# One ScalarE copy for two PSUM tiles, and one broadcast product for four, in a gated delta rule

## What is computed

```python
decay = jnp.exp(jnp.where(causal, gc[..., :, None] - gc[..., None, :], -jnp.inf))
kb = k * beta[..., None]
lower = jnp.where(strict, jnp.einsum('nhcid,nhcjd->nhcij', kb, k) * decay, 0.0)
uw = lax.linalg.triangular_solve(lower, rhs, left_side=True, lower=True, unit_diagonal=True)
...
kd = k * jnp.exp(g_last[..., None] - gc)[..., None]
v_new = u_c - jnp.einsum('nhik,nhkv->nhiv', w_c, state)
state = state * a_c[..., None, None] + jnp.einsum('nhjk,nhjv->nhkv', kd_c, v_new)
```

## The kernel before

| step | level 2 | level 3 | level 4 | level 5 |
|---|---|---|---|---|
| 0 | 2 | 3 | 1 | 2 |
| 1 | 1 | 2 | 3 | 0 |
| 2 | 1 | 0 | 1 | 3 |
| 3 | 0 | 1 | 2 | 3 |
| 4 | 0 | 3 | 0 | 2 |
| 5 | 0 | 2 | 3 | 0 |
| 6 | 1 | 3 | 1 | 2 |
| 7 | 3 | 1 | 1 | 1 |

## Time and profile before

### The profile page before, as it was taken

One profiled execution on the slowest core, in us unless ns is written; L12 is line 12 of the kernel. 1 busy time (PEld: TensorE's weight loads), 2 busy tenths in 40 slices (PEclk: granted clock), 3 DMA queues, 4 the chain that ended last, 5 costly groups with the idle time before them and its releaser, 6 DMA issues. The chain is left out here.

```text
span 3287.1 us, 56382 instructions
## 1 busy us (share of the span) xinstructions
PE 3210.5 (98%) x23386; PEld 2744.4 (83%) x23386; DVE 1654.8 (50%) x2484; ACT 1286.7 (39%) x2064; POOL 62.5 (2%) x79
## 2 busy tenths in 40 slices
PE   8999999999999999999998999999999999999999
PEld 7997889889788988888887888788888888876899
DVE  7744574774457552223674667542233323247444
ACT  5433454544345452223543444432223222234433
POOL 0000000000000010000000000000000000000000
PEclk9999999999999999999999999999999999999999
DMA  6545654454655432222221333222222222211353
GB/s 260 180 167 220 227 189 169 180 179 157 253 205 180 178 116 102 93 99 90 103 78 64 131 118 131 79 103 90 102 90 90 90 102 90 102 64 39 129 180 127
DMA packets 62918, 439.27 MB, mean 134 GB/s; under 512 B 6672, under 2 KB 9872, under 8 KB 10000
## 3 DMA queue, kind: packets, MB, share of 16 engines
q1 hardware_dynamic: 61552, 435.43, 36.7%
q10 hardware_dynamic: 1184, 1.18, 0.1%
HBM read 435.54 MB, written 1.05 MB: 133 GB/s over the span
## 5 line engine op out<-in xcount | busy, mean ns | idle before, releaser
L701 ACT ACTIVATE sb_w_split<-sb_ring 128x2048 fp32r<-128x2048 f32 x263 | 504.2, 1917 | 905.4 <-PE ps_low L465 706.0
L709 DVE TENSOR_TENSOR sb_w_split<-sb_ring,sb_w_split 128x2048 fp32r<-128x2048 f32 x263 | 603.3, 2294 | 432.3 <-ACT sb_w_split L701 432.3
L465 PE MATMUL ps_low<-sb_x_split,sb_w_split 128*128 128x512 f32 (+1 forms) x3520 | 691.3, 355 | 18.6 <-DVE sb_w_split L735 13.4
L465 PE MATMUL ps_high<-sb_x_split,sb_w_split 128*128 128x512 f32 (+1 forms) x3520 | 685.2, 353 | 1.9 <-DVE sb_w_split L709 1.9
L465 PEld LDWEIGHTS ps_low<-sb_x_split,sb_w_split 128*128 128x128 f32 x3520 | 579.5, 189 | 119.6 <-DVE sb_w_split L735 13.4
L465 PEld LDWEIGHTS ps_high<-sb_x_split,sb_w_split 128*128 128x128 f32 x3520 | 580.1, 189 | 96.8 <-DVE sb_w_split L709 2.9
L465 PE MATMUL ps_low<-sb_a_split,sb_w_split 128*128 128x256 f32 (+1 forms) x2112 | 370.2, 325 | 0.0
L465 PE MATMUL ps_high<-sb_a_split,sb_w_split 128*128 128x256 f32 (+1 forms) x2112 | 368.2, 323 | 0.0
L465 PEld LDWEIGHTS ps_low<-sb_a_split,sb_w_split 128*128 128x128 f32 x2112 | 314.2, 190 | 37.6 <-DVE sb_w_split L709 2.8
L465 PEld LDWEIGHTS ps_high<-sb_a_split,sb_w_split 128*128 128x128 f32 x2112 | 314.2, 190 | 30.4
L465 PE MATMUL ps_low<-sb_xn,sb_ring 128*128 128x256 f32 (+1 forms) x800 | 184.3, 388 | 0.5 <-ACT sb_xn L2652 0.5
(11 more groups left out here) (376 smaller groups left out, 3181.0 us busy)
## 6 DMA issues: line engine op xcount, KB each, us to landing
sb_ring<-weights SPq DMA_DIRECT2D x411, 1024.0 KB, 4.8
sb_consts<-consts SPq DMA_DIRECT2D x1, 2020.0 KB, 14.9
sb_h<-xT SPq DMA_DIRECT2D x1, 1024.0 KB, 6.9
sb_h<-ctxT ACTq DMA_DIRECT2D x1, 1024.0 KB, 20.8
out<-sb_h SPq DMA_DIRECT2D x1, 1024.0 KB, 4.8
sb_vectors<-vectors SPq DMA_DIRECT2D x1, 269.0 KB, 2.9
sb_arena<-positions ACTq DMA_DIRECT2D x1, 128.0 KB, 7.1
```

The lines of the kernel that those rows point to most:

```text
L465: ins = self.g.nc.tensor.matmul(out, lhsT, rhs, start=start, stop=stop)
L701: g.nc.scalar.activation(g.w_split[:, 0, s % 2, :], g.ring[:, n % SLOTS, :], ACT.Copy).then_inc(g.sem["w_high"], 1)
L709: g.nc.vector.tensor_tensor(g.w_split[:, 1, s % 2, :], g.ring[:, n % SLOTS, :], g.w_split[:, 0, s % 2, :].bitcast(F32), ALU.subtract).then ...
```

## The change

The four banks of a side become one PSUM tensor of four banks, at the same place, and `banks` is a list of views of it. In the levels 2 to 5 ScalarE copies both directions' tiles in one operation of 2x256 elements on 128 partitions, once for the transposed pair and once for the product pair. It waits for both tiles and increases `low_free` by two at its end. Where the pair begins in bank 3 it would wrap around, and the two copies stay. VectorE's key operand becomes one product with the factor broadcast along the tokens' width.

```diff
-        self.banks = {s: [ctx.enter_context(nc.psum_tensor(f"ps_{s}{i}", [P, 512], F32)) for i in range(4)]
-                      for s in ("low", "high")}
+        self.psum = {s: ctx.enter_context(nc.psum_tensor(f"ps_{s}", [P, 4, 512], F32)) for s in ("low", "high")}
+        self.banks = {s: [self.psum[s][:, i, :] for i in range(4)] for s in ("low", "high")}
...
+    def copy_two(into):
+        at = act.tiles["low"] % 4
+        if at == 3:
+            for d in range(2):
+                act.wait_ge(g.sem["low_full"], act.tiles["low"] + 1)
+                A(into[:, d, :], act.tile("low")[:, 0:GH * HALF], ACT.Copy).then_inc(g.sem["low_free"], act.frees("low"))
+            return
+        act.wait_ge(g.sem["low_full"], act.tiles["low"] + 2)
+        act.tile("low")
+        act.tile("low")
+        A(into, g.psum["low"][:, at:at + 2, 0:GH * HALF], ACT.Copy).then_inc(g.sem["low_free"], act.frees("low") + act.frees("low"))
...
     for level in range(2, LEVELS - 1):
-        for d in range(2):
-            act.wait_ge(g.sem["low_full"], act.tiles["low"] + 1)
-            A(b["turned"][:, d, :], act.tile("low")[:, 0:GH * HALF], ACT.Copy).then_inc(g.sem["low_free"], act.frees("low"))
-        to_product(0)
-        to_product(1)
+        copy_two(b["turned"])
+        copy_two(b["product"][:, :, 0:GH * HALF])
...
-        per_head(dve, lambda h, c: v.tensor_scalar(b["k_out"][:, d, c], tile[:, c], head_column(b, "key_decay", s, d, h), None, ALU.mult),
-                 lambda ins: ins.then_inc(g.sem["high_free"], dve.frees("high")))
+        decay = b["key_decay"][:, CHUNK_ORDER[d][t], d, head:head + GH].rearrange("p (h o) -> p h o", o=1).to_broadcast([P, GH, P])
+        v.tensor_tensor(heads_view(b["k_out"][:, d, :]), heads_view(tile[:, :]), decay, ALU.mult).then_inc(
+            g.sem["high_free"], dve.frees("high"))
```

## The result

The changed kernel takes 3294.91 us (median of 20 runs, 3287.94 to 3299.10) against 3287.88 us for the kernel before (20 runs, 3281.93 to 3294.63): a ratio of 1.0022, with a 95% interval of 1.0016 to 1.0028. That is +7.0 us by the medians, +5.3 to +9.2 us by the interval, and it lies astride the 0.2% (6.6 us) that I had set as the least that can be told from no change. I had forecast +4.8 us, between +2.8 and +6.5. The absolute figure of 3295.4 came closer than the difference did, only because the median of before fell from 3290.6 us over three runs to 3287.9 over twenty: 3294.91 lies inside the 3293.4 to 3297.1 that I had given, while +7.0 lies 0.5 us above the upper end of the differences, and its interval lies on both sides of that end.

A forecast was written before the change was run, and what follows sets the result against it. TensorE bounds the kernel, its extra tile waiting for the bank freed by a level's first copy. Delays of 4.98 us less 0.2 swallowed give +4.8 us, 3295.4 us from 3290.6; range 3293.4 to 3297.1 (+2.8 to +6.5), 60 in 100.

The forecast's parts named there:

- What bounds the kernel: TensorE, busy 98%; in levels its extra tile waits for the bank freed by the first transposed copy, 0.44 us after its start.
- The length of the merged copy: ScalarE's copy of the transposed pair, 2x256 elements: taken as 0.60 us, bounds 0.50 and 0.76, against 0.381 for one.
- the two-bank copy costs as two copies: Rival: merged copy takes 0.76 us, delay 0.41 us in 20 levels, 8.3 us slower, 3298.9 us; 5 in 100.
- The wait for the second tile: Transposed pair: second tile full two matmuls later, 0.035 us; bank freed 0.25 us later, or 0.22 where ScalarE was late.
- How often: Of 32 levels, 17 lose 0.25 us, 3 lose 0.22 and one 0.07: 4.98 us longer.
- the 0.07 us: Level 4 of step 0: extra tile already 0.62 us behind the copy, so the new distance of 0.69 costs 0.07.
- The product pair and the key operand at nothing: Merged product copies in 22 levels and 12 key operands: each taken as 0; gains at most 1.3 us and 0.3 us.
- The stalls: TensorE's 8 "issue" gaps of about 1 us may swallow delays: at most 2.0 us, one counted, -0.2 us.
- The delay and lost clock: Rival: longer TensorE idle times bring new 1.2 GHz spells, 1.5 us each; two give 7.9 us, 3298.5 us; 12 in 100.
- Faster by more than 0.2%: Rival: all VectorE's 5.2 us and ScalarE's 2.8 us on the path, 3282.6 us, or low-clock spells vanish; 3 in 100.
- ScalarE's time counts after all: Rival: TensorE waits for the last copy, so 46 merges gain 2.8 us; 3287.5 us with VectorE's 0.3; 4 in 100.
- What would show it: Signs: extra tile 0.66 to 0.76 us behind merged copy, 0.44 with bank 3; steps 4.8 us longer; over 20 copy waits.

The follow-up runs named there:

- The late release: Kernel before, no copy merged; the first transposed copy no longer frees its bank, the second frees both: 3299.66 us, ratio 1.0032, +11.4 us.
- the extra tile on the other side: Changed kernel, merging kept, with the extra tile (half unit, sum, key product) on PSUM's "high" side: 3285.41 us, ratio 0.9991 against the kernel before.
- the four with the early release: Kernel before (3287.88 us), only product pair merged (3287.84), only key operand changed (3288.74), changed kernel with two transposed copies put back (3288.25).
- the three with a late one and no filler: Changed kernel (3294.91 us), kernel before with only the transposed pair merged (3295.01), kernel before with both banks freed by the second single copy (3299.66).
- the extra tile on "high": Three kernels with the extra tile in "high" banks: kernel before 3284.64 us, changed kernel 3285.41, changed kernel with transposed pair in two copies 3286.16.
- the kernel before with the long filler: Kernel before plus one idle matmul of 256 columns ahead of each extra tile in levels 2 to 5: 3300.46 us, ratio 1.0033, +10.8 us.

## Why the prediction came out as it did

**What bounds the kernel.** Right. TensorE sets the time; 5 us less of VectorE's work brought nothing that the runs can tell. The copy that TensorE feels is the first of a level, and it is felt through its bank. The late release, without any merging, and the extra tile on the other side, with it, show this from both sides.

**The length of the merged copy.** Taken at 0.60 us between bounds of 0.50 and 0.76; measured 0.596. The rival "the two-bank copy costs as two copies" is out. The trace of before gives two copies as 0.66 us, and the new one is 0.06 us shorter, as taken.

**The wait for the second tile.** This is the step that failed, by its size: the term "so two are 0.035 us". I took the second tile to be full two weight loads after the first. Measured, the merged copy starts 0.12 us later than the first of two did (0.85 against 0.73 us behind the transposes, by the median of the merged levels). The bank is free 0.12 + 0.21 = 0.33 us later, not 0.25. The semaphore events of level 2 of step 0 divide the 0.12 us: the second tile signals 0.06 us behind the first (0.765 and 0.706 us behind the transposes, in both kernels), and the merged copy starts 0.08 us behind its signal where the first of two started 0.02 us behind its own. What makes up that second 0.06 us was not tried. It belongs to the wait and not to the read over two banks: in the three levels behind a table load, where both tiles had long been full, the merged copy starts where the first of two did, 1.94 us behind the transposes.

**How often.** 17 levels at full cost, 3 at 0.22 us, and two of step 0 held by TensorE itself. The 17 and the 3 are right (the earlier trace rows moved by 0.21). In level 4 of step 0 I had let TensorE absorb all but 0.07 us. There the extra tile was 1.35 us behind the transposes before:

```profile
1824.90 0.69 PE L465 MATMUL ps_low<-sb_consts,sb_xn 64*64 64x64 f32 x32
```

and is 1.67 us behind them in the changed kernel, 0.32 us later:

```profile
1821.36 0.69 PE L465 MATMUL ps_low<-sb_consts,sb_xn 64*64 64x64 f32 x32
...
1822.20 0.60 ACT L3604 ACTIVATE sb_xn<-ps_low 128x512 f32<-128x512 f32 x1
...
1822.76 0.34 PE L465 MATMUL ps_low<-sb_xn 64*64 64x64 f32 x7 [0.32 <-issue]
...
1823.03 1.08 PE L465 MATMUL ps_low<-sb_ring,sb_cond_act 128*32 128x128 f32 x32
```

But it is not the copy that held it: TensorE had a stall of 0.32 us within its own products. The kernel with only the transposed pair merged had none of that length there:

```profile
1822.19 0.69 PE L465 MATMUL ps_low<-sb_consts,sb_xn 64*64 64x64 f32 x32
...
1823.69 1.08 PE L465 MATMUL ps_low<-sb_ring,sb_cond_act 128*32 128x128 f32 x32
```

Its extra tile is 1.50 us behind the transposes and the level 0.15 us longer than before, and in the late release it is 0.10 us longer. So the absorption was as I had said, and the 0.07 us had only inherited the delay that was too small. Level 5 of step 0 absorbed it, as I had said (1.56 us before, 1.59 after). The sum of the delays with the measured terms is 17 x 0.33 + 3 x 0.21 + 0.15 + 0.03 = 6.4 us (6.6 with the stall of the changed kernel's profile), where I had 4.98. By what is left of the stretch, the two kernels with the merged transposed pair lie 6.7 us above the four with the early release (274.3 and 267.6).

**The product pair and the key operand at nothing.** Right, each by a kernel of its own: +0.2 us (-3.3 to +4.3 by the ratio's interval) and -0.8 us (-3.0 to +3.3). Gains of 1.3 us, or of the 0.3 us that I kept as a bound, can't be told from zero in these runs. The forecast duration of 0.69 us was right, and VectorE's waits for TensorE grew by more than its gain.

**The stalls.** I counted -0.2 us for one gap that swallows its delay, with at most 2.0. In the table the four kernels with an early release have 8.5 to 12.3 us of stalls, the three with a late one and no filler 7.0 to 8.7: on average 10.6 and 7.7. One profile of each is not enough for a size, and what ends a stall is still in no row. That the delays are partly swallowed, by more than I had counted, is likely and not shown.

**The delay and lost clock.** I gave it 12 in 100 and priced a new spell at 1.53 us, with two needed to decide. One place fits it: level 4 of step 4, where low clock came in all three profiles with a late release and cost, within the level, the 1.53 us that I had taken from the earlier trace rows in two of them and 0.9 us in the late release, where it began later. The other two places of long idle time did not change that way, so from the profiles one added spell is likely and not shown. The mean granted clock of the whole span was 0.99345 in the 20 runs of the changed kernel, against 0.99424 in 87 runs of the kernel before (those beside the experiments). Within those 87 runs, all of one program, the time rises by 2.4 us for each 0.001 of clock lost, so 0.0008 stands for 1.9 us. The other two kernels with a late release and no filler also ran at a lower mean clock than the runs of before beside them: by 0.0008 (transposed pair only) and 0.0017 (late release), while the six that release early or have the extra tile on "high" lie between 0.0002 lower and 0.0007 higher (the standard error of such a difference is about 0.0004). So a later release goes with a lower clock, for some 2 to 4 us, more than one spell at one place would give. What brings it about is open: the kernels with the extra tile on "high" had 13.6 to 20.6 us at 1.2 GHz in the stretch, and the kernel before with the long filler 17.1, none of it at these three places. Most of the low clock comes from something that no row names.

**The sum of it.** 6.4 to 6.6 us of delays, some 3 us of stalls taken off and some 1.5 to 2 us of clock added make 5 to 5.5 us. Measured were +7.0 us by the medians and by the means of the 20 runs on either side, and +5.3 by the means against the 87 other runs of before. The first term is measured to some tenths; the two others are estimates from few profiles, and up to 2 us between them and +7.0 stay unexplained. My 4.8 us thus had a first term that was about 1.5 us too small, and two that I had set near zero and that partly cancel. That it came as near as it did is in part luck.

**Faster by more than 0.2%; ScalarE's time counts after all.** Both out. ScalarE has the 46 instructions fewer, and the part with 24 of them alone makes the kernel slower by 6.9 us.

**What would show it.** I had said 0.66 to 0.76 us from copy to extra tile (measured 0.65, and 0.74 with the sum), 0.44 in the bank-3 levels (measured 0.44, and 0.53 with the sum, as before), 24 and 22 merged copies at 0.60 us, over 20 waits for the transposed copy (measured 19), and 12 key operands at 0.69 us. For the length of the steps I had said 4.8 us more. The profiled pair shows 3.2 us, with 5.2 us less of stalls and 3.3 us more at 1.2 GHz; with both taken out, 6.7. The granted clock from 1811 to 2110 us is 0.98 in both profiles.

## What to carry to other kernels

Before two PSUM evictions are merged into one, look for who needs the first bank: a merged copy starts when the second tile is full and frees the first bank when both are read. The time saved on the copying engine (46 x 0.06 us here) is worth nothing if that engine waits anyway, and the later release was paid in full by the engine that bounds the kernel. A start that kept one distance to a copy's end, whatever the waiting engine did before, was a bank wait here even though it showed up as only a few tenths of a microsecond, and moving the waiting tile to banks that are long free was worth 5 us here (1.3 to 7.6), where all that merging could have given was 2.8 us. And when single profiles disagree with the medians, take the low clock and the stalls out of the stretch before reading its length.

## What the hardware showed that I had not expected

- Waiting for the second of two tiles whose last matmuls are two instructions apart cost 0.12 us, not the 0.035 us of two weight loads by their mean time in the stream: the two signals are 0.06 us apart, and the copy starts 0.06 us later behind its signal.
- One program on one core varies by over 10 us from run to run (3281.9 to 3294.6 us in 20 runs), and the time follows the mean granted clock (correlation -0.83 over 87 runs, 2.4 us for 0.001). In two profiles of kernels whose instructions are the same up to there, the stretch of all work ahead of level 2 of step 0 took 1811.2 and 1821.2 us, at clocks of 1.00 and 0.99:

```profile
0.00:1811.23 1811.23, 1776.46 (x10992) 1531.11 (x10993) 992.54 (x1388) 775.09 (x1201) 62.57 (x79) 1.00 0.44 159
```

```profile
0.00:1821.20 1821.20, 1785.57 (x10993) 1538.56 (x10993) 992.07 (x1388) 775.46 (x1201) 62.57 (x79) 0.99 0.44 158
```

  So a single pair of runs can't show a difference of 7 us, and the profiled pair had the wrong sign.
- The Trainium skill ("ScalarE: Activation LUTs", What ACT_TABLE_LOAD costs) gives 186 ns + 0.833 ns per element for a copy with immediate operands, an estimated 612 ns for 512 elements. The trace's 596 ns for a copy over two banks is near it. Its 93 ns of overlap back to back would make the merge worth 0.09 us; the trace has 0.06.
- The step from 1.30 to 1.51 or 1.58 us of idle time in one place was followed by a fall of the granted clock from 1.00 to 0.76 in three profiles of three, against none of four before it; with work of no use put into that idle time the clock stayed at 1.00 there in three of three. But 1.51 and 1.58 us in step 2 were followed by a fall in one profile of three only, against two of four at 1.30 us, and 1.42 and 1.49 us in step 6 in none. One place isn't enough to make a rule of it.
